# One hybrid mLSTM / sparse-attention / mixture-of-experts layer: the meta rows of four memory heads put side by side, and the closing residual sum split differently between VectorE and TensorE

## The reference, cut to what matters

```python
w = jnp.exp(d_mat - m_t[..., None]) * jnp.einsum('bhtd,bhsd->bhts', q, k)   # decay times score
num = a[..., None] * jnp.einsum('bhvk,bhtk->bhtv', c_st, q) + jnp.einsum('bhts,bhsv->bhtv', w, v)
den = a * jnp.einsum('bhk,bhtk->bht', n_st, q) + w.sum(-1)
h = num / jnp.maximum(jnp.abs(den), jnp.exp(-m_t))[..., None]
```

```python
for e in range(N_EXPERTS):
    he = jax.nn.silu(hf @ w_gate[e]) * (hf @ w_up[e])
    y = y + combine[:, e:e + 1] * (he @ w_down[e])
...
h = _layer_norm(DN_ALPHA * h + _moe(...), ln2_g[l], ln2_b[l])
```

## Time and profile before

| | us |
|---|---|
| median of 3 runs | 789.19 |
| lowest and highest run | 787.22, 789.69 |
| profiled execution, its own time | 788.36 |
| span of the profiled execution | 785.8 |

### The profile page before, as it was taken

How to read it: one execution, slowest core, us unless ns; L and a number is a source line. 1 busy time by engine, 2 the same in 40 slices (tenths; PEclk the granted TensorE clock), 3 DMA queues, 4 the chain that set the end, 5 groups by cost and what they waited for, 6 DMA issues and landing times.

```text
span 785.8 us, 10936 instructions
## 1 busy us (share of the span) xinstructions
PE 737.2 (94%) x4030; PEld 600.3 (76%) x4032; DVE 597.8 (76%) x832; ACT 431.8 (55%) x513; POOL 79.9 (10%) x113
## 2 busy tenths in 40 slices
PE   3899999999999999999999688999999999999993
PEld 3877999986777777878888466888888888888871
DVE  6967999796864445523766789898899899899878
ACT  4643242346555445742220514787778878878745
POOL 6010000000110000000001111111112111212001
PEclk9999999999999999999999868999999999999997
DMA  9675223410363111342179856999999999999162
GB/s 260 169 218 183 88 73 94 156 54 1 114 266 106 55 54 55 108 161 97 64 216 408 297 177 211 339 395 397 397 389 405 392 402 391 399 399 365 62 237 107
DMA packets 104702, 172.16 MB, mean 219 GB/s; under 512 B 20860, under 2 KB 41596, under 8 KB 104472
## 3 DMA queue, kind: packets, MB, share of 16 engines
q1 hardware_dynamic: 94784, 152.84, 54.6%
q0 software_dynamic: 4608, 12.92, 4.2%
q10 hardware_dynamic: 5272, 5.90, 2.4%
HBM read 161.32 MB, written 21.10 MB: 232 GB/s over the span
## 4 chain that ended last, share of the span: by engine, by line
PE 87%; DVE 8%; ACT 3%; issue 1%; ACTq 1%; POOL 0%; DVEq 0%; POOLq 0%
PE low L1129 17%; PE low L1130 16%; PE low L1131 16%; PE wide L1129 8%; PE wide L1131 8%; PE wide L1130 8%; PE wide L1532 2%; PE low L1411 1%; PE low L1371 1%; PE wide L1342 1%; PE wide L1545 1%; PE low L1539 1%; DVE m_lo L1983 1%; DVE slots L2081 1%; ACTq L730 1%
## 5 line engine op out<-in xcount | busy, mean ns | idle before, releaser
L1983 DVE TENSOR_TENSOR m_lo<-m_raw,m_hi 128x2048 fp32r<-128x2048 f32 x95 | 215.0, 2290 | 30.3 <-ACT m_hi L990 29.6
L990 ACT ACTIVATE m_hi<-m_raw 128x2048 fp32r<-128x2048 f32 x95 | 179.6, 1918 | 24.2 <-PE low L1131 23.8
L1129 PE MATMUL low<-m_hi,xe_hi 128*128 128x512 f32 x256 | 103.9, 406 | 1.0 <-DVE xe_lo L2059 0.6
L1131 PE MATMUL low<-m_hi,xe_lo 128*128 128x512 f32 x256 | 101.3, 396 | 0.0
L1130 PE MATMUL low<-m_lo,xe_hi 128*128 128x512 f32 x256 | 100.8, 394 | 0.0
L1129 PE MATMUL low<-hT_hi,w_hi 128*128 128x512 f32 (+1 forms) x240 | 94.6, 394 | 3.9 <-DVE hT_lo L1717 2.5
L1681 DVE TENSOR_TENSOR w_lo<-raw,w_hi 128x2048 fp32r<-128x2048 f32 x28 | 64.1, 2290 | 38.2 <-ACT w_hi L725 38.0
L1130 PE MATMUL low<-hT_lo,w_hi 128*128 128x512 f32 (+1 forms) x240 | 92.2, 384 | 0.0
L1131 PE MATMUL low<-hT_hi,w_lo 128*128 128x512 f32 (+1 forms) x240 | 91.6, 381 | 0.0
L725 ACT ACTIVATE w_hi<-raw 128x2048 fp32r<-128x2048 f32 x28 | 53.5, 1909 | 16.5 <-PE wide L1131 8.3
L1129 PEld LDWEIGHTS low<-m_hi,xe_hi 128*128 128x128 f32 x256 | 48.8, 190 | 13.7 <-DVE m_lo L1983 3.0
(11 more groups left out here) (402 smaller groups left out, 1408.6 us busy)
## 6 DMA issues: line engine op xcount, KB each, us to landing
m_raw<-in_w_gate SPq DMA_DIRECT2D x32, 1024.0 KB, 8.7
m_raw<-in_w_up SPq DMA_DIRECT2D x32, 1024.0 KB, 8.2
m_raw<-in_w_down SPq DMA_DIRECT2D x31, 1024.0 KB, 9.1
raw<-in_w_in SPq DMA_DIRECT2D x19, 1024.0 KB, 5.2
raw<-in_w_out SPq DMA_DIRECT2D x4, 1024.0 KB, 5.1
y<-y_dram SPq DMA_DIRECT2D x8, 512.0 KB, 6.6
table_dram<-table_row ACTq DMA_DIRECT2D x1, 2624.0 KB
strips<-table_dram SPq DMA_DIRECT2D x8, 264.0 KB, 4.2
```

Source lines behind the costliest of these rows:

```text
L990: nc.scalar.activation(m_hi[n % MS][:, :], (m_spare if is_last(n, j) else m_raw[slot])[:, :], ACT.Copy).then_inc(q["m_hi_ready"], 1)
L1129: nc.tensor.matmul(outp, lh, rh, start=first, stop=False)
L1131: return nc.tensor.matmul(outp, ll, rh, start=False, stop=last)
L1983: v.tensor_tensor(m_lo[n % MS][:, :], (m_spare if is_last(n, j) else m_raw[n % MR])[:, :], m_hi[n % MS][:, :].bitcast(F32), ALU.subtract). ...
```

## The change

Three things.

- **Meta rows.** Head h's 16 meta keys go to partitions 32h to 32h + 15 of one tile, so that one tile `dw_meta` (128 x 512) serves all heads: one exponential, one score step of four matmuls that write 32 partitions each, one multiplication. For that, the meta values go through `dw_meta` and four DMAs to their partitions, the negated maxima of the four heads come by a fifth DMA (`negm_meta`), all issued by ScalarE, and the biases by four one-column matmuls. Rows that carry nothing get the bias -1e30. GpSimd writes the constants early and its two later memsets fall away. Within a head the decays are made from the last tile of keys to the first.
- **Last expert.** The transposes of `hid` go ahead of those of `last_sel`, in two halves in two banks, each copied and subtracted by itself.
- **Closing stage.** VectorE makes `y1 = weight2 * y2 + y1` as a second instruction after the first; TensorE adds `y1` with the plain identity; `combine` falls away, and statistics and gain read the banks. The last tile's last pass and its store are cut into halves.

```diff
@@ ScalarE @@
-            nc.scalar.activation(v_ext[0:META, TT, :, 0:P], bank[3][0:META, :].rearrange("p (x y) -> p x y", x=MH), ACT.Copy).then_inc(q["vm_ready"], 1)
+            nc.scalar.activation(dw_meta[0:META, :], bank[3][0:META, :], ACT.Copy).then_inc(q["vm_ready"], 1)
+            act.wait_ge(q["vm_ready"], 1)
+            for h in range(MH):
+                act.dma_start(v_ext[32 * h:32 * h + META, TT, h, 0:P], dw_meta[0:META, h * P:(h + 1) * P]).then_inc(q["meta_loaded"], 16)
...
+            act.dma_start(negm_meta[:, :], bass.AP(tensor=negm_row.tensor, offset=negm_row.offset, ap=[[S, MH], [0, 32], [1, S]])).then_inc(q["meta_loaded"], 16)
...
             act.wait_ge(q["ut_ready"], 1)
+            act.wait_ge(q["meta_loaded"], 80)
+            nc.scalar.activation(dw_meta[:, :], negm_meta[:, :], ACT.Exp, bias=u_tok[:, 0, 0:1]).then_inc(q["d_ready"], 1)
...
-                    nc.scalar.activation(dw[0:META, h % 2, DOFF[TT]:DOFF[TT] + S], negm[0:META, h, :], ACT.Exp,
-                                         bias=u_tok[0:META, 0, h:h + 1]).then_inc(q["d_ready"], 1)
...
-            hd_hi_out(NE - 1)
+            for half in range(2):
+                act.wait_ge(q["hd_done"], NE + half)
+                nc.scalar.activation(hd_hi[:, 2 * half:2 * half + 2, :], bank[3 - half][:, 0:2 * P].rearrange("p (c x) -> p c x", c=2), ACT.Copy).then_inc(q["hd_hi_ready"], 1)
...
-                step(nc.scalar.activation(y1[:, i, :], h1[:, i, :], ACT.Copy, accum_out=total2[:, i:i + 1]))
+                step(nc.scalar.activation(y1[:, i, :], total_of(i)[:, :], ACT.Copy, accum_out=total2[:, i:i + 1]))
@@ TensorE @@
-            for i in range(TT + 1):
...
+            for h in range(MH):
+                nc.tensor.matmul(bank[2][32 * h:32 * h + 32, 320:321], rows[64:68, 1, 0:32], ident[64:68, 64 + h:65 + h], start=True, stop=True)
...
+            for h in range(MH):
+                mm = nc.tensor.matmul(bank[4][32 * h:32 * h + 32, :], kT[:, h, 0:32], qT[:, h, META:T], start=True, stop=True)
+            mm.then_inc(q["st_done"], 1)
...
-                    nc.tensor.matmul(bank[4][0:META, :], kT[:, h, 0:META], qT[:, h, META:T], start=True, stop=True)
...
-                        nc.tensor.matmul(oo, dw[:, g % 2, DOFF[TT] + i * P:DOFF[TT] + (i + 1) * P], v_ext[:, TT, g, :], start=True, stop=False)
+                        nc.tensor.matmul(oo, dw_meta[:, i * P:(i + 1) * P], v_ext[:, TT, g, :], start=True, stop=False)
...
-                pe.wait_ge(x_loaded[i], 48)
+                pe.wait_ge(q["part_ready"], 2 * i + 2)
                 for half in range(2):
-                    nc.tensor.matmul(pair[:, half * 512:half * 512 + 512], second_w[:, i, :], y2[:, i, half * 512:half * 512 + 512], start=True, stop=False)
+                    nc.tensor.matmul(pair[:, half * 512:half * 512 + 512], ident[:, :], y1[:, i, half * 512:half * 512 + 512], start=True, stop=False)
@@ VectorE @@
+            v.scalar_tensor_tensor(out=dw_meta[:, :], in0=bank[4][:, :], scalar=float(P ** -0.5), in1=dw_meta[:, :], op0=ALU.mult, op1=ALU.mult).then_inc(q["w_ready"], 1)
...
-                v.scalar_tensor_tensor(out=wm, in0=bank[4][0:META, :], scalar=scale, in1=wm, op0=ALU.mult, op1=ALU.mult).then_inc(q["w_ready"], 1)
...
-                v.tensor_tensor(h1[:, i, :], (wide[1], low[0], low[1], wide[0])[i][:, :], y1[:, i, :], ALU.add).then_inc(q["combined"], 1)
...
-                step(v.scalar_tensor_tensor(out=h1[:, i, :], in0=h1[:, i, :], scalar=negmu2[:, i:i + 1], in1=g2[:, :], op0=ALU.add, op1=ALU.mult))
+                step(v.scalar_tensor_tensor(out=h1[:, i, :], in0=total_of(i)[:, :], scalar=negmu2[:, i:i + 1], in1=g2[:, :], op0=ALU.add, op1=ALU.mult))
```

More of the change, by code:

```diff
@@ L541, in _ @@
                 results_load()
-            for i in range(TT):
+            for i in range(TT - 1):
                 sp.wait_ge(q["out_ready"], i + 1)
                 sp.dma_start(out[0, i * P:(i + 1) * P, :], h1[:, i, :]).then_inc(q["out_stored"], 16)
-            sp.wait_ge(q["out_stored"], 16 * TT)
+            for half in range(2):
+                sp.wait_ge(q["out_ready"], TT + half)
+                sp.dma_start(out[0, (TT - 1) * P:TT * P, half * 512:half * 512 + 512], h1[:, TT - 1, half * 512:half * 512 + 512]).then_inc(q["out_stored"], 16)
+            sp.wait_ge(q["out_stored"], 16 * (TT + 1))
         @block.gpsimd
@@ L886, in _ @@
                         act.wait_ge(q["block_done"], B_NUM + 2 * (h - 1))
-                    for j in range(TT):
+                    for j in reversed(range(TT)):
                         u = u_tok[:, 1 + j, h:h + 1]
@@ L1275, in _ @@
             pe.wait_ge(q["side_out"], 4)
-            for i in range(TT + 1):
-                n, lo = (P, META + (i - 1) * P) if i else (META, 0)
-                nc.tensor.transpose(bank[2][0:n, 320 + 4 * i:324 + 4 * i], rows[64:68, 1, lo:lo + n], ident[64:68, 64:68])
+            for h in range(MH):
+                nc.tensor.matmul(bank[2][32 * h:32 * h + 32, 320:321], rows[64:68, 1, 0:32], ident[64:68, 64 + h:65 + h], start=True, stop=True)
+            for i in range(TT):
+                nc.tensor.transpose(bank[2][:, 324 + 4 * i:328 + 4 * i], rows[64:68, 1, META + i * P:META + (i + 1) * P], ident[64:68, 64:68])
             for i in range(TT):
@@ L1610, in _ @@
             m_unit(u + 5, 0, bank[1][:, :], 1, xe_hi, xe_lo)
+            pe.wait_ge(q["hid_ready"], NE)
+            for half in range(2):
+                for c in range(2):
+                    mm = nc.tensor.transpose(bank[3 - half][:, c * P:(c + 1) * P], hid[:, (2 * half + c) * P:(2 * half + c + 1) * P], ident[:, :])
+                mm.then_inc(q["hd_done"], 1)
             pe.wait_ge(q["sel_ready"], 1)
@@ L1616, in _ @@
             mm.then_inc(q["sel_done"], 1)
-            hidden(NE - 1)
-            pe.wait_ge(q["hd_lo_ready"], NE)
             pe.wait_ge(q["y_out"], NE)
-            m_unit(u + 6, 1, bank[4][:, :], None, hd_hi, hd_lo)
+            pe.wait_ge(q["m_lo_ready"], u + 6)
+            wh, wl = (t[1][:, :].rearrange("p (c n) -> p c n", c=4) for t in (m_hi, m_lo))
+            for k in range(4):
+                pe.wait_ge(q["hd_lo_ready"], NE + k // 2)
+                mm = product(bank[4][:, :], (hd_hi[:, k, :], hd_lo[:, k, :]), (wh[:, k, :], wl[:, k, :]), k == 0, k == 3)
+            mm.then_inc(q["m_used"], 1)
             m_unit(u + 7, 2, bank[5][:, :], None, hd_hi, hd_lo)
@@ L1826, in _ @@
             dve.wait_ge(q["ut_done"], 1)
-            step(v.tensor_copy(u_tok[0:META, 0, :], bank[2][0:META, 320:324]))
+            dve.wait_ge(q["const_done"], 3)
+            step(v.tensor_tensor(u_tok[:, 0, 0:1], bank[2][:, 320:321], u_tok[:, 0, 1:2], ALU.min))
             step(v.tensor_copy(u_tok[:, 1:, :], bank[2][:, 324:340].rearrange("p (i x) -> p i x", i=TT)))
@@ L2176, in _, with part @@
             hidden_out(NE - 1, MU * NE - 2)
-            v.tensor_tensor(second_w[:, :, :], ident[:, :].rearrange("p (o x) -> p o x", o=1).to_broadcast([P, TT, P]),
-                            weight[:, 1, :].rearrange("p (i o) -> p i o", o=1).to_broadcast([P, TT, P]), ALU.mult).then_inc(q["sel_ready"], 2)
-            hd_lo_out(NE - 1)
+            for half in range(2):
+                dve.wait_ge(q["hd_hi_ready"], NE + half)
+                v.tensor_tensor(hd_lo[:, 2 * half:2 * half + 2, :], bank[3 - half][:, 0:2 * P].rearrange("p (c x) -> p c x", c=2),
+                                hd_hi[:, 2 * half:2 * half + 2, :].bitcast(F32), ALU.subtract).then_inc(q["hd_lo_ready"], 1)
             m_split_lo(MU + 5, j)
-            def part(i):
+            def part(i, done, count):
                 dve.wait_ge(x_loaded[i], 48)
-                return v.scalar_tensor_tensor(out=y1[:, i, :], in0=y1[:, i, :], scalar=weight[:, 0, i:i + 1], in1=h1[:, i, :], op0=ALU.mult, op1=ALU.add)
+                v.scalar_tensor_tensor(out=y1[:, i, :], in0=y1[:, i, :], scalar=weight[:, 0, i:i + 1], in1=h1[:, i, :], op0=ALU.mult, op1=ALU.add).then_inc(done, 1)
+                dve.wait_ge(done, count + 1)
+                v.scalar_tensor_tensor(out=y1[:, i, :], in0=y2[:, i, :], scalar=weight[:, 1, i:i + 1], in1=y1[:, i, :], op0=ALU.mult, op1=ALU.add).then_inc(done, 1)
             def last_lo(half):
```

89 lines of the change are left out of this document (44 added, 45 removed).

## The result

| | before | after |
|---|---|---|
| median of 4 runs each, us | 788.21 | 780.38 |
| lowest and highest run | 786.43, 789.69 | 780.05, 781.75 |
| profiled execution, its own time | 788.36 | 780.10 |
| its span | 785.8 | 777.7 |

A forecast was written before the change was run, and what follows sets the result against it. The chain of waits, 87% on TensorE, was taken as the bound: 2.4 us from the memory branch plus 2.4 from last expert and closing stage, 4.8 off 788.36, gave 783.6, put at 784.0; range 781.8 to 787.5.

The forecast's parts named there:

- Four heads' scores: Memory branch: score matmuls of four heads at once take 1.16 us, 0.20 more than the 0.96 replaced.
- part A: Memory branch, 182 to 215 us: meta rows of all heads together gain 2.4 us, bounds -0.3 to 2.9.
- Head 1's scores: Memory branch: one head's meta scores, on the chain of waits at 191.40, fall away, gaining 0.96 us.
- The issues: Memory branch: ScalarE's five DMA issues take 0.36 us each, 1.8 in all, inside 4.4 us of cover, so cost nothing.
- The rival of dear issues: Memory branch: ScalarE's five DMA issues take 2.0 us each, 5.7 more than the cover; 789.7 us; chance 0.03.
- Carried to the end unchanged: Between memory branch and last expert: the memory branch's gain reaches the end whole, as later work starts from semaphores.
- lost on the way: After the memory branch: its gain is lost as waits and short clock falls lie otherwise; 785.5 to 787 us; chance 0.11.
- Part B: Last expert's activations: first product moves from 756.94 to 756.3, 0.64 us gained, bounds 0.3 and 1.0.
- Part C: Closing stage, 762 us to the end: VectorE sets the end, its last instruction ending at 780.7 instead of 782.76.
- The store: End of closing stage: storing 256 KB instead of 512 KB last saves 0.3 us, between nothing and 1.3.
- Serial groups: Memory branch: column groups run one after another, scores taking 3.84 us instead of 1.16; 786.7 us; chance 0.08.
- Clock in the closing stage: Closing stage: TensorE's clock falls after its wait in sum 0, sums take 5.2 us instead of 2.64; 789.9; chance 0.07.

The follow-up runs named there:

- the kernel with part A alone: Only the meta rows of four heads together, on the kernel before: 784.64 us median of 10, ratio 0.9955.
- the run with both forms: Kernel after with four extra score matmuls in one column group ahead of the four in four groups: 785.32 us in one execution.

## Why the prediction was wrong, point by point

The direction, the mechanisms and the bound of each stage held. What failed is the size of terms of the sum: what four heads' scores and the biases add, what head 1's scores give back, the wait and the branch of VectorE in the closing stage, and the store. Together they were 1.4 us short, and the first comparison added some 1.6 us, most of it chance. Taken from the mean of before, 788.3, the 6.2 us of the touched stretches make 782.1, inside the range; what lies beyond is that last part. By the touched stretches of undisturbed traces the change gives +0.15 - 3.05 - 0.65 - 2.0 - 0.6 = 6.2 us; I had 4.8.

- **Four heads' scores.** Forecast 1.16 us, measured 1.00, so 0.04 on top of one head's 0.96 and not 0.20. The router's row was the right form but not the right price: its 0.036 us a piece holds for 128 columns; 512 columns cost 0.125 and not four times 0.036. *Biases:* 0.15 for a forecast 0.3. Together 0.3 of the 0.5 us that part A was short (2.4, measured 2.9).
- **Head 1's scores.** I took out 0.96 us, the length of the meta step itself. From the last gate matmul ahead of it to the first sums of head 0 (rows below, before and then after) it was 3.55 us and is 2.39: 1.16 us. The step from the gate matmul to the scores went from 0.32 to 0.23, and that from the scores of the real keys to the sums from 2.26 to 2.16. These 0.2 us are the rest of part A; why each is shorter is not shown.

```profile
191.01 0.39 PE L1131 MATMUL low<-hT_hi,w_lo 128*128 128x512 f32 x1
...
192.30 2.42 PE L1294 MATMUL wide<-qT,kT 128*128 128x512 f32 x8
194.56 0.39 PE L1306 MATMUL low<-v_ext,dw 128*128 128x129 f32 x2
...
190.72 0.40 PE L1148 MATMUL low<-hT_hi,w_lo 128*128 128x512 f32 x1
190.95 2.32 PE L1314 MATMUL wide<-qT,kT 128*128 128x512 f32 x8
193.11 0.39 PE L1326 MATMUL low<-v_ext,dw_meta 128*128 128x129 f32 x2
```

- **The issues.** Priced at 0.36, measured 0.63. The choice of the row was wrong; the named cover was real and took it, with 1.2 us to spare. The rival of dear issues (from 0.87 us each) was nearer than its chance of 0.03 says.
- **Carried to the end unchanged.** Right for the change, and the kernel with part A alone shows it. The rival "lost on the way" had the right cause, falls of the clock that lie otherwise, and the wrong sign here. The stretch from 486 us stood near 0.50 in the kernel before (row below), its counterpart, 483 to 486 in the rows of after above, at 1.00; from `v_h` to the second expert's `hid` that execution of after is 1.1 us shorter. I had this as a possibility below my own case and put only one fall of 1.65 us there.

```profile
486.00:490.00 4.00, 4.00 (x11) 3.14 (x12) 3.95 (x3) 2.31 (x3) 0.00 (x0) 0.57 1.01 343
```

- **Part B.** 0.64 forecast, 0.60 measured at the first product and 0.65 at the end of the last weight tile, shown by itself.
- **Part C.** 1.42 forecast, 2.0 measured (21.58 to 21.78 us closing in the traces without a late load, 23.67 to 23.71 before). Two terms of the sum were too dear. I let tile 1 start at 761.2, 2.8 us behind tile 0, because of its load; it starts 2.52 us behind (753.59 to 756.11), so 0.3 us. The load was not moved, as I had said: its first issue stands 0.24 us ahead of `hid` in both traces (753.61 and 748.65). But I took the 7.6 us that it needed in one trace as fixed; in the seven traces in which VectorE waited for it, it needed 7.3 to 8.9. That it was in time here is in part luck. And I added 0.3 us for the branch behind `yl_lo`, 1.7 us from the first `yl_lo` to tile 2; it is 1.32 (758.63 to 759.95), as tile 2's pass starts 0.08 before `yl_lo` ends: where VectorE has work, that gap is not there. The two make up the whole 0.6 within 0.1.
- **The store.** 0.3 forecast between 0 and 1.3, measured 0.6, shown by putting it back.
- **The rivals.** Serial groups: out, by the run with both forms. Clock in the closing stage: it happens, in one of the six profiled executions with exactly this closing stage and, just ahead of it, in one of the four with that of before, for 1 to 1.5 us. It was a matter of single executions, not of the kernel. (My sum for it gives 6.1 us and not 5.9, and leaves out VectorE's gain pass behind the last variance.)
- **The range.** It was built from the sum's bounds and one fall of the clock. The spread of single executions of 1.4 us, with medians of four on each side, belonged in it as well; the mean over all executions, 781.6 against 788.3, is 0.2 us below its lower edge.

## What to carry to other kernels

When a change is worth under 1%, cut both traces at instructions that they share and add up only the stretches that the change touches; a difference elsewhere is chance until the same kernel, run again, keeps it. Do not take the landing time of a load from one trace as fixed: the one of tile 1 needed 7.3 to 8.9 us. And before taking work from an engine that is never idle, look at when all its inputs come: here `yl_hi` and the last load followed so closely that one pass less was worth nothing.

## What the runs showed of the hardware

- Matmuls that write different groups of 32 columns overlapped almost fully: four fp32 ones of 512 columns took 1.00 us, in one group 3.41 us, and one alone 0.96.
- A DMA issue of ScalarE of this form took 0.63 us, another form later in the kernel 0.36.
- Short falls of the granted clock to 0.50 came at places that differ between executions of one program (472.7 and 486, then 481 and 757), and a stretch with TensorE busy in 0.96 of 3 us was passed over while one with 1.57 of 3 was followed by a fall. A longer fall, behind idle time at 443 to 450 us, came in all fourteen and lasted 10 to 21 us.
- A store of 256 KB landed in 2.0 us, one of 512 KB in 2.6.
